# Laying out the DRAM scratch of PEER gates by unit instead of by token chunk

## The reference, cut to what matters

```python
def peer(h, wq, k1, k2, u, v):
    q = (xt @ wq).reshape(T, PEER_HEADS, 2, PEER_HALF)
    s1 = jnp.einsum("thd,hnd->thn", q[:, :, 0], k1)
    s2 = jnp.einsum("thd,hnd->thn", q[:, :, 1], k2)
    ...                                  # top 16 of each, top 16 of their sums
    experts = e1 * N_KEYS + e2
    gates = jax.nn.softmax(best, axis=-1)
    a = jnp.einsum("td,thkd->thk", xb, u[eb])
    act = gb * jax.nn.gelu(a)
    return jnp.einsum("thk,thkd->td", act, v[eb])
```

## Time and profile before

| | us |
|---|---|
| median of 3 runs | 3128.13 |
| lowest, highest | 3126.65, 3140.87 |
| profiled execution, its own time | 3137.47 |
| its span in the trace | 3135.7 |

### The profile page before, as it was taken

One profiled execution on the slowest core, in us unless ns is written; L12 is line 12 of the kernel. 1 busy time (PEld: TensorE's weight loads), 2 busy tenths in 40 slices (PEclk: granted clock), 3 DMA queues, 4 the chain that ended last, 5 costly groups with the idle time before them and its releaser, 6 DMA issues.

```text
span 3135.7 us, 41987 instructions
## 1 busy us (share of the span) xinstructions
PE 2998.2 (96%) x17373; PEld 2759.4 (88%) x17373; DVE 2533.5 (81%) x3098; ACT 1030.0 (33%) x1081; POOL 839.7 (27%) x380
## 2 busy tenths in 40 slices
PE   5799989989989999999999999989999999999999
PEld 3687765557778899999999999989999999999999
DVE  7986968756673589999988998854989899898985
ACT  4323243341122333333333333323333334333331
POOL 5600000000030013333123333421444444444440
PEclk8999989989999999999999999999999999999999
DMA  9722223347744468888778988987999999999994
GB/s 368 268 94 77 81 85 138 124 168 302 290 159 180 142 228 326 333 333 321 274 266 343 356 346 337 389 330 285 375 395 389 390 392 392 395 386 398 385 399 164
DMA packets 182257, 893.82 MB, mean 285 GB/s; under 512 B 15680, under 2 KB 77248, under 8 KB 85824
## 3 DMA queue, kind: packets, MB, share of 16 engines
q1 hardware_dynamic: 111376, 491.29, 42.4%
q0 software_dynamic: 46080, 335.56, 26.2%
q10 hardware_dynamic: 24624, 64.45, 5.3%
HBM read 836.71 MB, written 54.53 MB: 284 GB/s over the span
## 4 chain that ended last, share of the span: by engine, by line
PE 84%; DVE 10%; DMA 2%; ACT 2%; issue 1%; SPq 0%; ACTq 0%; DVEq 0%; PEldq 0%
PE bank L1909 10%; PE bank L1911 10%; PE bank L1910 10%; PE bank L1968 10%; PE bank L1969 10%; PE bank L1970 10%; PE bank L1606 3%; PE bank L1608 3%; PE bank L1607 3%; DVE ada_w L944 2%; PE bank L1944 2%; PE bank L1843 2%; PE bank L1844 2%; PE bank L1845 2%; DMA ada_w<-wada 1%
## 5 line engine op out<-in xcount | busy, mean ns | idle before, releaser
L475 POOL DMA_INDIRECT u_row<-u_rows,urow_i x128 | 285.6, 2231 | 823.7 <-DVE u_row L1374 559.0
L1909 PE MATMUL bank<-act_hi,w_hi 128*128 128x352 f32 x1376 | 447.7, 325 | 8.0 <-DVE low L906 8.0
L1910 PE MATMUL bank<-act_lo,w_hi 128*128 128x352 f32 x1376 | 445.0, 323 | 0.0
L1968 PE MATMUL bank<-wt_hi,w_hi 128*128 128x352 f32 x1360 | 439.5, 323 | 4.9 <-DVE w_lo L906 4.4
L1969 PE MATMUL bank<-wt_lo,w_hi 128*128 128x352 f32 x1360 | 438.4, 322 | 0.0
L1911 PE MATMUL bank<-act_hi,low 128*128 128x352 f32 x1024 | 332.1, 324 | 0.0
L1911 PE MATMUL bank<-act_hi,w_lo 128*128 128x352 f32 x1024 | 330.3, 323 | 0.0
L1970 PE MATMUL bank<-wt_hi,w_lo 128*128 128x352 f32 x1024 | 330.3, 323 | 0.0
L1970 PE MATMUL bank<-wt_hi,low 128*128 128x352 f32 x1024 | 329.3, 322 | 0.0
L486 POOL DMA_INDIRECT u_row<-v_rows,urow_i x96 | 232.2, 2418 | 271.3 <-DVE y_g L1521 249.5
L1374 DVE SCALAR_TENSOR_TENSOR u_row<-u_row,h2t 128x2048 f32<-128x2048 f32 x128 | 288.9, 2288 | 13.4 <-DMA u_row<-u_rows,urow_i 13.3
(11 more groups left out here) (340 smaller groups left out, 7234.3 us busy)
## 6 DMA issues: line engine op xcount, KB each, us to landing
ada_w<-wada SPq DMA_DIRECT2D x80, 1024.0 KB, 5.5
w_raw<-u SPq DMA_DIRECT2D x64, 1024.0 KB, 5.9
raw<-u SPq DMA_DIRECT2D x64, 1024.0 KB, 5.6
w_raw<-v SPq DMA_DIRECT2D x64, 1024.0 KB, 9.1
raw<-v SPq DMA_DIRECT2D x64, 1024.0 KB, 6.8
w_raw<-win SPq DMA_DIRECT2D x27, 1024.0 KB, 4.9
gelu_scratch<-gelu_s ACTq DMA_DIRECT2D x128, 176.0 KB, 8.4
gate_scratch<-g_chunk ACTq DMA_DIRECT2D x11, 2048.0 KB, 12.2
```

Of the source, the lines that this page charges most:

```text
L475: pool.indirect_dma_start(u_row[n % 3][:], None, urow_d, bass.IndirectOffsetOnAxis(ap=col, axis=0)).then_inc(u_row_loaded[n % 3], 16)
L1909: pe.matmul(out, wh[:, k, :], HD(k), start=(k == 0), stop=False)
L1910: pe.matmul(out, wh[:, k, :], LD(k), start=False, stop=False)
L1968: pe.matmul(o, wh[:, 8 * e + d, :], th, start=begin is not None and e == 0, stop=False)
```

## The change

`gate_d` gets another order of its dimensions. Before, it is [chunk of 32 tokens (11), partition (128), row (128), token in chunk (32)]; after, [partition (128), unit (32), chunk (11), row in unit (4), token in chunk (32)]. The innermost 4 x 32 floats, 512 B, stand together in both. Reading one unit took 11 x 128 runs of 512 B before and takes 128 runs of 5632 B after. Storing one chunk took 128 runs of 16384 B before and takes 128 x 32 runs of 512 B after. Nothing else changes: no instruction of PE, DVE, ACT or POOL, no wait, no order of issue, no byte count, and the layouts in the on-chip buffers are the same.

```diff
-    gate_d = nc.dram_tensor("gate_scratch", [TD // GC, P, NKEY, GC], F32).ap()
+    gate_d = nc.dram_tensor("gate_scratch", [P, NKEY // 4, TD // GC, 4, GC], F32).ap()
...
                 sp.dma_start(wt[:], gelu_d[:, rows, :]).then_inc(wt_loaded, 16)
-                sp.dma_start(gate_l[:], gate_d[:, :, rows, :].rearrange("c p i t -> p c i t")).then_inc(wt_loaded, 16)
+                sp.dma_start(gate_l[:], gate_d[:, n]).then_inc(wt_loaded, 16)
...
                         act.wait_ge(g_copied[g], LEAD + t + 1)
-                    act.dma_start(gate_d[chunk], g_chunk[cb][:]).then_inc(g_stored[cb], 16)
+                    act.dma_start(gate_d[:, :, chunk], g_chunk[cb][:].rearrange("p (n i) t -> p n i t", i=4)).then_inc(g_stored[cb], 16)
```

## The result

The changed kernel takes 3169.68 us (median of 6 runs, 3167.05 to 3175.59); the kernel before, run beside it again, 3139.73 (6 runs, 3126.65 to 3141.86). The ratio is 1.0114, 95% interval 1.0098 to 1.0131: slower by 1.1%, beyond the 0.5% that can be told, and outside the predicted 3108 to 3148. The profiled execution of the changed kernel took 3168.95 us, its span is 3167.2, that of before 3135.7: 31.5 us to explain.

What follows compares the result with a forecast made beforehand. PE bounds the kernel, and gate loads cost at most 24.3 us through its three gaps and clock. Loads -4.6 and stores +3.0 give about -2 on the 3128.1 median: 3126 us, range 3108 to 3148.

Steps and rivals of the forecast that it cites:

- What bounds the kernel: PE's idle gaps of 8.0, 5.0 and 4.4 us at unit gate loads, plus 6.9 of clock: 24.3 us at most.
- Part 1, the loads: Unit gate loads in longer runs land earlier at units 0, 1 and 3, shortening DVE's and PE's waits: -4.6 us.
- The sum: Whole kernel: -4.6 from the loads and +3.0 from the stores, -1.6, so about -2 us.
- Part 2, the stores on the DMA engines: Chunk stores at 27 to 32 ns per 512 B: +2.0 to +3.2 us each, free in hot stage, +3.0 after.
- rival B: 512 B writes above 34 ns overload the DMA engines in the hot stage: 3150 at 45 ns, 3188 at 61; chance 0.12.
- stall 1: PE's 8.0 us idle gap at unit 0's gate load; forecast 3.0 us longer by the stores, 2.0 gained by the load.
- Part 3, the issue: On ACT, issuing a 4096-run gate store takes 0.65 us, covered by ACT's 5.3 idle us.
- A: At the unit loads, gates land with wt and PE keeps its clock: -18 us, 3110; chance 0.15.
- C: In the DMA packets, the layout does not reach them, so nothing moves: 3128 us; chance 0.07.
- the hot stage shows PE gaps: Named sign that the prediction is wrong: PE idle in the hot stage, where the added store work was to cost nothing.

Runs made afterwards that it cites:

- e11: Kernel before, old layout, with the loads of unit 0 issued two raw blocks earlier, unit 1 one block, unit 3 one v block: 0.9922, 3112.0 us.
- e2: Against the kernel before: stores still 128 runs of 16 KB, each unit read as 128 runs of 5632 B (timing only): 0.9972.
- e5: The change with each chunk stored in four transfers of 1024 runs spread over four jobs; 0.9977 against the kernel before.
- e1: Stores as in the change, but units read again as 11 x 128 runs of 512 B (timing only); 1.0112 against the kernel before.
- e9: The change with each whole gate store issued one job later on ACT, just behind that job's gelu store; 1.0106 against the kernel before.
- e8: Kernel before, its layout too, with the loads of unit 0 issued two raw blocks earlier and of unit 1 one block earlier: 0.9950.
- e7: The change without POOL's row gathers 64 to 121, those of the hot stage (timing only); 1.0001 against the kernel before.

## Why the prediction was wrong, point by point

Of the 44 us between the forecast (3126) and the measured 3169.7, 11.6 are the base: I added to the median of three runs, 3128.1, and six runs give 3139.7. The other 32 are the mechanism, and against the right base too the forecast, no change, was wrong.

**What bounds the kernel: right.** PE's three gaps behind DVE's three waits for `gate_l` were read as all that the gate loads cost, 24.3 us with the clock; e11, which closes them to 2.2 us, gains 24.

**Part 1, the loads: right in sign and near in size.** The sum had -4.6 us, as 2.0, 1.2 and 1.4. The gaps shrink by 4.0 in the change and in e2 by 5.4, as 3.0, 0.9 and 1.6; e2 as a whole gains 8 to 9, so something that I left as it was, the clock or SP's two held issues, gives back too. The steady state shows the cheaper load and no gain, as said: the median landing of `gate_l` goes from 11.4 to 10.3 us, q1's share at 2330 to 2930 us is 45.5% (49.2% before at 2300 to 2900, 3 points forecast), and PE is busy 200 of 200 us in both.

**Part 2, the stores on the DMA engines: the price was right, the time to land was not.** In the changed kernel q10 takes, from 1642 to 2008 us:

```profile
q10 hardware_dynamic: 45769, 27.30, 24.0%
```

1405 us of engine time; ten gate stores are 20.97 MB, the other 6.3 MB are 4,500 gelu packets at 61 ns, 274 us; 1131 us for 40,960 packets is 28 ns each, forecast at 27 to 32, under the 34 from which rival B would have decided. The whole-run counts are as forecast (q1 111376 to 70416, q10 24624 to 68272 packets). That the stage has no loss by bandwidth is e5. But I had the stores land 2 to 4 us later, and in e1 they land 12 us later (23.9 against 12.2): 7 us of engine time are spread over 24. The +3.0 at stall 1 can't be read in the change, as PE comes there late; in e5 the price at unit 0 is 4.2 us. That this is near the 3.0 is luck as far as these runs show: it comes by the wait for the last store's landing, which I had not priced.

**Part 3, the issue: the step that failed.** I extrapolated the issue of a store of 4096 runs to 0.65 us (it is 0.52) and covered it with ACT's 5.3 idle us. That is the price of the instruction, and the wait that the change adds is at the next one: a gelu store that cannot be issued until enough of the gate runs ahead of it have drained. What was queued behind it on ACT (the high part, the copy of the gates) and who waits for that (PE) was never asked, because Part 3 had no wait in it. Measured: 81 us of hold-up, 22.1 us of PE idle in the hot stage and 8.7 behind it. The trace of before had a sign of it, which I did not read: the raw loads behind the gate loads of 1408 runs, 6.67 us behind unit 0's (above) and this one behind unit 1's:

```profile
2093.50 0.43 SPq L409 DMA_DIRECT2D gate_l<-gate_scratch  x1
2100.23 3.43 SPq L397 DMA_DIRECT2D raw<-u  x1
```

3.43 us for an issue of 0.33, with 88 runs per engine queued, and 256 were to come. At the two places the change, with 8 runs per engine, has 0.33, and e1, which reads in 512 B again, 4.96 and 4.76:

```profile
2131.49 4.76 SPq L397 DMA_DIRECT2D raw<-u  x1
```

**The rivals.** A did not come: the gates land nearer to wt, not with it. B had the right sign and the wrong mechanism: it priced the engines' bandwidth and put the decision at 34 ns per packet, and the loss came at 28. C is out by the packet counts. (What A supposed of the loads, that short runs fare badly beside other queues, fits the landings of the stores.) Of the signs of being wrong that I named, "the hot stage shows PE gaps" came, and nothing in Part 3 led to it: B had put it there for want of bandwidth.

**Left open.** How many runs a queue takes before it holds its issuer; whether gathers or any full traffic is what slows the stores; why the hold-ups vary from 2 to 19 us in one kernel; and why e9 drains more slowly.

## What to carry to other kernels

Price a transfer in many short runs at the next transfer on the same queue, and ask what its issuing engine has to do behind that: beside other traffic the issuer stood for up to 19 us here. If the short runs cannot be avoided, spread them over several jobs, or issue them from a queue whose next transfer is wanted late; both took the loss of the hot stage away here with the same packets. And where a load is waited for at three places only, moving its issue earlier (24 us) was worth more than making it cheaper (9).

## What the runs showed of the hardware

- The issue of a 128 x 352 store from ACT took 0.33 us, and 2 to 19 us behind a store of 4096 runs of 512 B; behind 128 runs of 16 KB, the same bytes, never over 0.36 us.
- The hold-up was the queue's own: during ACT's 19.12 us from 2041.43 on, SP issued two raw loads without delay (0.33 us for the first of them, 8.01 from the start of the first to the end of the second, 7.7 of which are the distance of two jobs).
- The same on SP: a raw load behind a gate load of 1408 runs of 512 B took 6.67 and 3.43 us to issue (before, units 0 and 1), 4.96 and 4.76 in e1, 7.64 and 6.33 in e8, and 0.33 behind a gate load of 128 runs of 5632 B (change, e2).
- A store of 4096 runs of 512 B landed after 23.9 us beside gathers (median of e1) and after 9.7 without (e7); one of 128 runs of 16 KB beside gathers after 12.2 (before).
- By the estimates above a 512 B write took 28 ns of a DMA engine and a 512 B read 32, against 19 for the same bytes in runs of 16 KB: the short run itself was cheap.
